# Two transformer blocks on one core: paired attention heads in block 1, and a new order of VectorE's and ScalarE's work around the linears behind it

## Time and profile before

| | us |
|---|---|
| median of 3 runs (1427.66 to 1428.82) | 1428.05 |
| the profiled execution | 1429.47 |
| its span, first to last instruction | 1426.9 |
| TensorE busy with matmuls | 1392.8 (98%) |
| VectorE / ScalarE / GpSimd busy | 991.8 / 692.8 / 397.8 |
| mean granted clock of TensorE | 0.992 |

### The profile page before, as it was taken

The page is one execution under the profiler, slowest core; times in us unless marked ns, Lnnn a source line. Parts: engine busy times, 40 slices in busy tenths (PEclk is TensorE's granted clock), DMA queues, the critical chain, the costliest instruction groups (busy, mean ns, idle before and its releaser), DMA issues.

```text
span 1426.9 us, 28045 instructions
## 1 busy us (share of the span) xinstructions
PE 1392.8 (98%) x11486; PEld 1361.6 (95%) x11486; DVE 991.8 (70%) x2241; ACT 692.8 (49%) x1188; POOL 397.8 (28%) x186
## 2 busy tenths in 40 slices
PE   6999999999999999999999999999999899899998
PEld 6888899999999999999999999999999889899998
DVE  3573435759998888999976666776667753777643
ACT  5554546545454444444443333333345655666653
POOL 3635456578800000000000000000000543584442
PEclk9999999999999999999999999999999999999999
DMA  7424235555665444444456766665665434455563
GB/s 276 143 75 133 88 108 178 176 165 178 189 193 180 148 149 148 149 148 149 148 176 190 230 190 191 188 186 189 191 187 170 148 119 121 150 172 178 183 199 107
DMA packets 65095, 234.99 MB, mean 165 GB/s; under 512 B 7228, under 2 KB 7612, under 8 KB 64968
## 3 DMA queue, kind: packets, MB, share of 16 engines
q1 hardware_dynamic: 64968, 233.20, 51.6%
HBM read 232.13 MB, written 1.05 MB: 163 GB/s over the span
## 4 chain that ended last, share of the span: by engine, by line
PE 89%; DVE 5%; ACT 4%; issue 1%; DMA 0%; POOL 0%; SPq 0%; DVEq 0%; ACTq 0%
PE PS L534 89%; ACT SPL L965 2%; DVE SPL L1344 1%; PE PS L656 1%; DMA RAW<-in_dense 0%; DVE ub L1999 0%; DVE HF L1361 0%; DVE ub L1996 0%; DVE ub L2003 0%; ACT ub L1311 0%; DVE HXb L1373 0%; DVE PS L1387 0%; DVE HS L1366 0%; POOL SPL L2026 0%; ACT HS L990 0%
## 5 line engine op out<-in xcount | busy, mean ns | idle before, releaser
L965 ACT ACTIVATE SPL<-RAW 128x1024 fp32r<-128x1024 f32 x432 | 454.4, 1058 | 561.1 <-PE PS L534 558.4
L2026 POOL TENSOR_TENSOR SPL<-RAW,SPL 128x1024 fp32r<-128x1024 f32 x150 | 367.3, 2451 | 1012.3 <-ACT SPL L965 1011.9
L534 PE MATMUL PS<-HS,SPL 128*128 128x256 f32 x4656 | 571.4, 282 | 15.7 <-DVE SPL L1344 15.7
L534 PEld LDWEIGHTS PS<-HS,SPL 128*128 128x128 f32 x4656 | 554.3, 189 | 18.5 <-issue 16.9
L1344 DVE TENSOR_TENSOR SPL<-RAW,SPL 128x1024 fp32r<-128x1024 f32 x282 | 350.0, 1243 | 233.6 <-ACT SPL L965 232.2
L534 PE MATMUL PS<-asp,SPL 128*128 128x256 f32 x3072 | 358.7, 279 | 0.0
L534 PEld LDWEIGHTS PS<-asp,SPL 128*128 128x128 f32 x3072 | 358.5, 188 | 0.1
L534 PE MATMUL PS<-HXb,SPL 128*128 128x256 f32 x720 | 91.9, 288 | 5.5 <-DVE SPL L1344 4.6
L534 PEld LDWEIGHTS PS<-HXb,SPL 128*128 128x128 f32 x720 | 88.5, 191 | 7.7 <-DVE SPL L1344 4.8
L1719 DVE TENSOR_SCALAR oh<-CC,T3f 128x128 f32<-128x128 f32 x256 | 87.7, 343 | 0.0
L1718 DVE TENSOR_SCALAR oh<-CC,T3f 128x128 f32<-128x128 f32 x256 | 72.0, 281 | 0.0
(11 more groups left out here) (253 smaller groups left out, 1175.1 us busy)
## 6 DMA issues: line engine op xcount, KB each, us to landing
RAW<-in_dense SPq DMA_DIRECT2D x176, 512.0 KB, 3.6
RAW<-in_eu SPq DMA_DIRECT2D x128, 512.0 KB, 3.6
RAW<-in_ev SPq DMA_DIRECT2D x128, 512.0 KB, 4.3
bias<-in_nab SPq DMA_DIRECT2D x2, 768.0 KB, 8.4
XT<-in_xT SPq DMA_DIRECT2D x4, 256.0 KB, 6.5
out_y<-HF SPq DMA_DIRECT2D x4, 256.0 KB, 2.4
c<-in_c SPq DMA_DIRECT2D x1, 960.0 KB, 7.2
c<-in_c SPq DMA_DIRECT2D x1, 512.0 KB, 5.3
```

The lines of the kernel that those rows point to most:

```text
L534: return e.matmul(out, l, r, start=start, stop=stop, skip_group_check=skip)
L965: e.activation(spl(n)[0], raw(n), ACT.Copy).then_inc(*up("act_high", ("hi", n)))
L2026: e.tensor_tensor(lo, raw(n), hi.bitcast(f32), ALU.subtract).then_inc(*up("pool_low", ("lo", n)))
```

## The change

In block 1's attention the rounds n = 0, 2, 4, 6 take the scores of two heads, the odd rounds from 3 on the transposes of two, the even ones from 4 on the products with v of two. The matmuls of the two heads alternate: the scores read rows 0-63 and 64-127 and write two banks; the products write partitions 0-63 and 64-127 of one bank. `prob` and `probT` hold the heads of a pair side by side. For `out`, `pg` and `wo` VectorE evacuates chunk n before it splits slot n + 3 (`walk_late`). Slot 2 of w_in_2 goes from GpSimd to VectorE. In `second_steps` `pair`, ScalarE copies the two results and makes the deviation before its two splits, and VectorE makes the reciprocal before its two. In `up`, ScalarE puts one split in front of f and one inside it, and VectorE's splits come one f earlier. The rings `nat`, `rs2` and `wo` get other banks. The diff, cut to its core:

```diff
     if AFTER <= n < SLOT0["wo2"] + 2 * NE:
-        return n in (AFTER + 5, SLOT0["w_in2"] + 2 * NE + 1, SLOT0["w_in2"] + 2 * NE + 3)
+        return n in (AFTER + 5, *(SLOT0["w_in2"] + 2 * NE + i for i in (1, 2, 3)))
...
     for n in range(12):
         yield "ld", n
-        if 1 <= n <= 8:
-            yield "nm", n - 1
         yield "ev", n
-        if n < 8:
-            yield "sc", n
-        if 1 <= n <= 8:
-            yield "tp", n - 1
-        if 2 <= n <= 9:
-            yield "pv", n - 2
+        if n % 2 == 0 and n < 8:
+            yield "sc", n // 2
+        if n % 2 == 1 and 3 <= n <= 9:
+            yield "tp", (n - 3) // 2
+        if n % 2 == 0 and 4 <= n <= 10:
+            yield "pv", (n - 4) // 2
         if n:
             yield "dq", n - 1
         yield "sp", n
-        if n < 8:
-            yield "ex", n
+        if n % 2 == 0 and n < 8:
+            yield "ex", n // 2
+        if n % 2 == 1 and n <= 7:
+            yield "nm", n // 2
...
-                 "nat": (4, 0, 5, 1), "turn": (7,), "head": (6,), "scr3": (2, 3, 6), "mean": (2, 3), "mean2": (6, 4),
-                 "rs2": (6, 4, 0, 7), "wo": (5, 1, 4, 0), "end": (6,),
+                 "nat": (4, 5, 0, 1), "turn": (7,), "head": (6,), "scr3": (2, 3, 6), "mean": (2, 3), "mean2": (6, 4),
+                 "rs2": (6, 4, 5, 7), "wo": (0, 1, 4, 5), "end": (6,),
...
+        def probs_of(tag, i):
+
+            return prob[i // 2 % 2][:, 512 * (i % 2):512 * (i % 2) + 512] if tag == "na" else prob[i % 2]
+
+        def turned_of(tag, i):
+            p = probT[i // 2 % 2][:, 512 * (i % 2):512 * (i % 2) + 512] if tag == "na" else probT[i % 2]
+            return p.rearrange("p (c t) -> p c t", t=256)
...
+        def walk_late(cur, split, evac):
+
+            for n in range(8):
+                evac(n)
+                split(cur[0] + n + NSPL)
+            cur[0] += 8
+            cur[1] += 64
...
+                    ps = [take("scr1", "na", 2 * i + j, "s") for j in range(2)]
...
                     for a in range(2):
-                        t = mm(ps[:, a * 256:a * 256 + 256], qka[r:r + 64, i // 2, a * 128:a * 128 + 128],
-                               qka[r:r + 64, 4 + i // 2, :])
-                    t.then_inc(*up("pe_score", ("full", "na", i, "s")))
+                        for j in range(2):
+                            r = 64 * j
+                            t = mm(ps[j][:, a * 256:a * 256 + 256], qka[r:r + 64, i, a * 128:a * 128 + 128],
+                                   qka[r:r + 64, 4 + i, :])
...
+                    t.then_inc(*up("pe_score", ("full", "na", 2 * i, "s"), ("full", "na", 2 * i + 1, "s")))
                 elif what == "tp":
-                    turn_probs("na", "scr1", i, 1)
+                    turn_probs("na", "scr1", 2 * i, 1)
+                    turn_probs("na", "scr1", 2 * i + 1, 1)
                 elif what == "pv":
-                    w.wait_ge(*at("ev", "va", i // 4, 1))
-                    weighted("na", i, 2, lambda h, c: va[:, c, h * 64:h * 64 + 64])
+                    ps = take("pv", "na", i)
+                    w.wait_ge(*at("ev", "va", i // 2, 1))
+                    for c in range(2):
+                        for j in range(2):
+                            h = 2 * i + j
+                            w.wait_ge(*at("probT", "na", h, 0))
+                            t = mm(ps[64 * j:64 * j + 64, 0:256], va[:, c, h * 64:h * 64 + 64], turned_of("na", h)[:, c, :],
+                                   c == 0, c == 1, True)
+                    t.then_inc(*up("pe_value", ("weighted", "na", 2 * i), ("weighted", "na", 2 * i + 1), ("full", "na", i)))
...
+                    exps("na", 2 * i, 256, 0)
+                    exps("na", 2 * i + 1, 256, 0)
+                    if i == 3:
                         warm(ACT.Sqrt)
...
                 if what == "pair":
-                    step()
-                    step()
-                    std(3, ("bank7", "o"))
-                    warm(ACT.Exp, 61)
                     raw2(0)
                     raw2(1)
+                    std(3, ("bank7", "o"))
+                    step()
+                    step()
+                    warm(ACT.Exp, 61)
                 elif what == "lin":
...
-                if f == 0:
+                if f < 21:
...
-            step()
-            up_evac(1)
-            up_evac(3)
-            run(walk(cur, 40, 8, split, lambda n: up_evac(n + 4), True))
+            for f in range(22):
+                if f < 21:
+                    step()
+                up_evac(2 * f + 1)
...
-                if i >= 2:
-                    w.wait_ge(*at("turned", tag, i - 2, 2 if tag == "dl" else 0))
-                elif tag == "dl":
-                    w.wait_ge(*at("turned", "na", 6 + i, 0))
+                if tag == "na":
+                    if i >= 4:
+                        w.wait_ge(*at("turned", "na", i - 4, 0))
+                else:
+                    w.wait_ge(*at(*(("turned", "dl", i - 2, 2) if i >= 2 else ("turned", "na", 5 + 2 * i, 0))))
...
+                    for h in (2 * i, 2 * i + 1):
+                        w.wait_ge(*at("full", "na", h, "s"))
+                        w.wait_ge(*at("biased", h))
+                        prob_free("na", h)
+                        for a in range(2):
+                            t = e.scalar_tensor_tensor(probs_of("na", h)[:, a * 256:a * 256 + 256],
+                                                       psum("na", h, "s")[:, a * 256:a * 256 + 256], rsq[:, a, h:h + 1],
+                                                       bias_of(h, a), ALU.mult, ALU.add)
+                        t.then_inc(*up("dve_soft", ("masked", "na", h), ("ev", "na", h, "s")))
+                        maxima("na", h, 256, 0)
...
+                    shares("na", 2 * i, 256, 0)
+                    shares("na", 2 * i + 1, 256, 0)
+                elif what == "pv":
+                    take_value("na", i, ona)
...
-            run(walk(cur, 8, 8, split, residual("out", 1), pair=True))
+            walk_late(cur, split, residual("out", 1))
...
             rstd(2)
-            for n in range(9):
-                pg_add(n)
-                if n == 1:
-                    split(cur[0] + NSPL)
-                    split(cur[0] + NSPL + 1)
-                elif 1 < n < 8:
-                    split(cur[0] + n + NSPL)
-            cur[0] += 8
-            cur[1] += 64
+            walk_late(cur, lambda n: split(n) if n < SLOT0["w_in2"] + 2 * NE + 2 else None, pg_add)
+            pg_add(8)
             gained(3, 7)
             sum_up(3, 6)
             sum_up(3, 7)
+            split(SLOT0["w_in2"] + 2 * NE + 2)
...
                 if what == "pair":
-                    step()
-                    step()
                     rstd(3)
+                    step()
+                    step()
...
-            run(walk(cur, 8, 8, split, residual("wo", 4), pair=True))
+            walk_late(cur, split, residual("wo", 4))
...
                                     ALU.mult).then_inc(*up("dve_conv", ("scaled", f)))
                 if f:
                     act_low(f - 1)
-                else:
-                    split(cur[0] + 2 + NSPL)
-                for i in range(2):
-                    if f > 1 or f == i == 1:
-                        split(cur[0] + NSPL)
+                for _ in range(2):
+                    if f < 21:
+                        split(cur[0] + 2 + NSPL)
                     cur[0] += 1
                     cur[1] += 8
```

More of the change, by code:

```diff
@@ L666, in weighted @@
                 r = 64 * (i % 2)
-                pt = probT[i % 2].rearrange("p (c t) -> p c t", t=256)
+                pt = turned_of(tag, i)
                 for c in range(n):
@@ L1017, in exps @@
             def exps(tag, i, width, base):
-                s = prob[i % 2][:, 0:2 * width].rearrange("p (a w) -> p a w", a=2)
+                s = probs_of(tag, i).rearrange("p (a w) -> p a w", a=2)
                 b = statb[:, base + i, :]
@@ L1500, in dve_program @@
                 elif what == "sc":
-                    w.wait_ge(*at("full", "na", i, "s"))
-                    w.wait_ge(*at("biased", i))
                     w.wait_ge(*at("qfactor", 0))
-                    prob_free("na", i)
-                    for a in range(2):
-                        t = e.scalar_tensor_tensor(prob[i % 2][:, a * 256:a * 256 + 256],
-                                                   psum("na", i, "s")[:, a * 256:a * 256 + 256], rsq[:, a, i:i + 1],
-                                                   bias_of(i, a), ALU.mult, ALU.add)
-                    t.then_inc(*up("dve_soft", ("masked", "na", i), ("ev", "na", i, "s")))
-                    maxima("na", i, 256, 0)
+                    for h in (2 * i, 2 * i + 1):
[8 more added lines that the diff above has]
+                        maxima("na", h, 256, 0)
                 elif what == "nm":
-                    shares("na", i, 256, 0)
-                elif what == "pv" and i % 2:
```

(5 more changed lines are left out.)

31 lines of the change are left out of this document (14 added, 17 removed).

## The result

| | us |
|---|---|
| before, median of 5 runs on the same chip (1427.66 to 1429.49) | 1428.05 |
| after, median of 5 runs (1412.65 to 1415.93) | 1414.70 |
| ratio, 95% interval | 0.9902, 0.9889 to 0.9915 |
| the profiled execution of after; its span | 1414.68; 1412.6 |
| predicted; range | 1403.0; 1398 to 1412 |

The change saves 13.4 us, not 25, and the time lies 2.7 us above the range. TensorE's and the splits' lines have moved: L534 is now L551, L965 is L991, L1344 is L1372, GpSimd's split L2026 is L2049, and the product of `up` is now L2026 (VectorE).

What follows compares the result with a forecast made beforehand. TensorE bounds the kernel, busy 1392.8 of 1426.9 us. Savings 4.2 + 4.0 + 1.0 + 3.3 + 1.4 + 1.85 + 1.3 + 3.4 + 4.5 = 24.95 take 1429.47 to 1404.5, less 1.4 to the median: 1403.0 us, range 1398 to 1412.

Steps and rivals of the forecast that it cites:

- A: Block 1's attention: two heads' passes run side by side, saving 4.2 us on scores and 4.0 on values.
- B: `out`: VectorE's result ahead of its split shortens TensorE's idle time, saving 1.0 us (0 to 1.7).
- C: `pg`: VectorE's split comes earlier, behind `pg_add(0)`, removing TensorE's idle time; 3.3 us saved (0 to 3.4).
- D: `qk2`: w_in_2's slot 2 on VectorE and ScalarE's copies before its splits save 1.4 us (0 to 1.4).
- E: `nat`: a new ring gives banks read long before, removing an idle time; 1.85 us saved (0 to 1.85).
- F: `wo`: VectorE's sum first cuts the ring of waits with ScalarE; 1.3 us saved (0 to 1.6).
- G: `up`: earlier splits and one inside ScalarE's wait for the convolution; 3.4 us saved (0 to 3.4).
- H: Three half-clock stretches near the idle times of C, E and G go with them; 4.5 us saved (0 to 5.1).
- rivals 1 and 3: Attention pairs: column halves run serially, 1407.0, chance 0.15; matmuls keep strict order, five steps for four, 1404.8, chance 0.05.
- Rival 5: In `up`, ScalarE's second split and VectorE's splits lengthen the round; slower from 6.8 us, 1436 at 7.2; chance 0.02.
- Rival 2: B to G: idle times return at the next wait, half of 12.25 us; two half-clock stretches stay; 1412.1, chance 0.19.
- The last line of the prediction: Wrong if idle times go but TensorE's passes between lengthen, or a new releaser, GpSimd's split first, stands before them.

Runs made afterwards that it cites:

- e10: Kernel after with SiLU's result in PSUM and w_in_2's slot 4 on VectorE, then rings `nat`, `rs2`, `wo` put back as before: 1401.31 us.
- e4: Kernel after with the eight matmuls of a pair issued head by head instead of alternating, for scores and values: 1415.20 us.
- e2: Kernel after with `up`'s two slots per f exchanged between GpSimd and VectorE, VectorE's splits behind the product: 1406.26 us.
- e1: Kernel after with SiLU's result in `up` written to a free PSUM bank instead of SBUF: 1403.28 us.
- e6: e1 with `fk` 1 (twelve passes of K = 12) moved ahead of `vd` 3 in block 1: 1402.57 us.
- e7: Kernel after with only the order of `up` on ScalarE and VectorE put back as before: 1409.23 us.
- e8: Kernel before with SiLU's result in PSUM and nothing else changed: 1426.01 us, against 1428.29 on that chip.

## Why the prediction was wrong

By its own steps; gains measured in the profiles:

| part | predicted | measured | from |
|---|---|---|---|
| A pairs | 8.2 | 9.7 | first scores to the dilated norms, 57.91 to 130.88 before, 72.97; 56.93 to 120.18 after, 63.25 |
| B `out` | 1.0 | 1.3 | 1.68 of idle, now 0.40 |
| C `pg` | 3.3 | 3.2 | 3.38, now 0.18 |
| D `qk2` | 1.4 | -1.3 | 0.53 + 0.86, now 2.68 |
| E banks | 1.85 | 1.85 | e10 |
| F `wo` | 1.3 | 1.6 | 0.42 + 1.16, now none |
| G `up`, `dn`, clock included | 3.4 + 1.5 | -4.6 | 195.15, now 199.70 |
| H, the other stretches | 3.0 | 1.6 | two gone, 1.7 each; the one of block 1 3.5 us longer |

The column sums to 13.35, the distance of the medians; that it is so exact is luck, since the profiled executions differ by 14.8, of which 1.0 lies ahead of the first scores.

**A** was right, and both halves overlap: rivals 1 and 3 fall (e4). It gave 1.5 us more, since eight transposes in a row take 0.87 us (80.30 to 81.17) against 2 x 0.59, and the first pairs have fewer changes of group. VectorE kept up, as worked out.

**B, C, E, F** were right within 0.3 us each. (The sum comes to 1403.1, not 1403.0; nothing hangs on it.)

**G is the step that failed.** "With one split moved into the time in which ScalarE waits for the convolution (1.0 us), 5.2 to 5.5" counts ScalarE's ring and takes every VectorE duration from the trace of before. But a split of ScalarE starts GpSimd's split of the same slot, and the prediction did not follow it there. The change moved 2.4 us of GpSimd from beside the convolutions, where it costs VectorE nothing, to beside the product, where it costs 1.0: 6.02 us a late round where 5.2 to 5.5 was reckoned. Rival 5 had the right place and named VectorE's splits and the slot, not this; at 6.02 to 6.3 us the ring stayed below its 6.8. What it loses is more than 0.3 us a round: the last f ends late, TensorE waits 2.98 us at `dn`, and the clock falls to half for 3.4 us (1.7 lost).

**D** fell to the same thing. I used it in one direction, "the one before it took 2.57 us instead of 0.48, while GpSimd was splitting w_in_2's slot 2", and moved that slot to VectorE; I did not ask which instruction then stood beside the next GpSimd splits. The low part L1373 reads XT and HXb, both in SBUF, and ends at 1129.90, 0.28 us behind the split that runs from 1127.23 in the kernel before:

```profile
1127.23 2.39 POOL L2026 TENSOR_TENSOR SPL<-RAW,SPL 128x1024 fp32r<-128x1024 f32 x1 [2.97 <-ACT SPL L965]
```

So the rows held the rule, and I read them as a slowness of that instruction.

**H** took a link for certain that holds only sometimes. Behind the idle time in `dn` a stretch stands in all three profiles that have it (after, e4, e2). Behind the 2.7 us in `qk2` it stands in four of six (e1, e2, e4, e6; not in after or e7), and behind e7's 2.45 and e10's 1.85 there is none. e8's `pg` is that of the kernel before, with the same idle time, and keeps the full clock:

```profile
1109.90 14.24 PE L534 MATMUL PS<-HS,SPL 128*128 128x256 f32 x120 [3.38 <-DVE SPL L1344]
...
1110.70:1114.10 3.40, 3.40 (x32) 3.40 (x31) 2.68 (x5) 1.88 (x4) 1.32 (x1) 1.00 0.98 353
```

The same 120 passes took 15.90 us in the kernel before. So an idle time of 2 to 3 us may bring a stretch of 1.5 to 1.7 us or not, which fits a spread of the runs over 3.3 us, and H's 1.6 in the table is that of one pair of executions. What decides it is not shown.

**Rival 2** (1412.1) was the nearest, and the price it named, with "VectorE slows to 2.4 us for a 1.2 us split when GpSimd works beside it", was the cause that came, though not in the places that it counted. I gave it 0.19 and a flat half of the gains, where the order of starts around GpSimd's split would have given 1.0 us in each late round. The last line of the prediction named the sign, a new releaser with GpSimd first; it came as a VectorE instruction made longer, which the column of releasers does not show.

Part G missed another thing: the 5.73 us of a late round of before is not TensorE's. e1's rounds are 5.60, the same as 48 passes in `dn` before (1383.77 to 1389.37), so the old ring also cost 0.13 us a round.

## What to carry to other kernels

When a change moves one engine's work, move its followers too: write down for a whole round which instructions of VectorE have both inputs in SBUF, and where each GpSimd instruction starts and ends after the change, not before. If one stands under the other on a ring, put one input in PSUM (here 11.4 us for one operand) or let it be an instruction that nobody waits for. A group whose mean lies above its shape's usual time (1432 for 424 ns, 546 for 425) is the mark to look for, also in the kernel that one starts from.

## What I had not expected of the hardware

- Two heads on opposite row halves or opposite column halves cost TensorE what one does (1.06 and 1.02 us for eight passes, 1.05 and 1.01 for four), also when all passes of one half stand first in the kernel (1.07). The Trainium skill ("TensorE: Matmul & The Clock Gate", Part 3) says that matmuls start and end in program order; the run with head-by-head order speaks against it here.
- In the rows above, an instruction of VectorE with 256 columns and both inputs in SBUF that starts during a GpSimd split ends 0.28 us behind it, whether it is the product, a multiply or a low part. So its cost can be reckoned from the end of the split, and not as a factor on its own time.
- The clock fell to 1.2 GHz with TensorE busy all the time, behind 12 passes of K = 12 (2.85 us) and in 12 of K = 64, for 6.8 us in most profiles and 10.3 in one; with 24 full passes ahead of those of K = 64 it lasted 3.4. An idle time of 3.38 us was followed by such a fall in one execution and not in another. What exactly decides it stays open.
- The order of two instructions that do not depend on each other (product, GpSimd's split) and the memory of one operand decided 11 us of 1414 (e1).
